# A depthwise convolution of 31 taps: half of it as streamed matrices on TensorE, half summed in PSUM, and a layer norm about a pivot

## What is computed

```
def conformer_conv_module(h, w_pw1, b_pw1, w_dw, b_dw, ln_g, ln_b, w_pw2, b_pw2):
    a, g = jnp.split(h @ w_pw1 + b_pw1, 2, axis=-1)
    u = a * jax.nn.sigmoid(g)
    u = causal_depthwise_conv(u, w_dw) + b_dw      # 31 taps per channel, over the tokens
    u = jax.nn.silu(layer_norm(u, ln_g, ln_b))     # mean and variance over the 1024 channels
    return u @ w_pw2 + b_pw2
```

## Time and profile before

| what | us |
|---|---|
| median of 3 runs | 2044.67 (2043.39 to 2046.08) |
| the profiled execution: time, span from first to last instruction | 2046.26, 2044.4 |
| busy in it: TensorE, VectorE, GpSimd, ScalarE | 1964.0, 905.4, 1159.7, 440.5 |
| chain that ended last: TensorE, VectorE, ScalarE | 81%, 10%, 2% |
| mean granted clock of TensorE | 0.98 of full speed |

### The profile page before, as it was taken

The page is one execution under the profiler, slowest core; times in us unless marked ns, Lnnn a source line. Parts: engine busy times, 40 slices in busy tenths (PEclk is TensorE's granted clock), DMA queues, the critical chain, the costliest instruction groups (busy, mean ns, idle before and its releaser), DMA issues.

```text
span 2044.4 us, 24823 instructions
## 1 busy us (share of the span) xinstructions
PE 1964.0 (96%) x8961; PEld 1542.2 (75%) x8961; DVE 905.4 (44%) x1383; ACT 440.5 (22%) x954; POOL 1159.7 (57%) x648
## 2 busy tenths in 40 slices
PE   8999899999999999999999999997879999999998
PEld 6876567888888877877788888876657678888886
DVE  6345863543430055343543332118999453333202
ACT  3334641211110020033211110003253431111000
POOL 6963536766675556621676666646610367666662
PEclk9999999999999999999999999999989999999999
DMA  5431002223233213210243233222210123333311
GB/s 193 133 115 32 1 1 83 82 92 94 93 121 99 76 46 100 93 42 13 71 115 101 93 104 110 85 73 63 72 31 0 35 69 113 92 92 108 109 61 41
DMA packets 42376, 160.85 MB, mean 79 GB/s; under 512 B 4928, under 2 KB 5184, under 8 KB 42304
## 3 DMA queue, kind: packets, MB, share of 16 engines
q1 hardware_dynamic: 41472, 157.74, 24.8%
q10 hardware_dynamic: 832, 2.11, 0.3%
HBM read 157.73 MB, written 2.10 MB: 78 GB/s over the span
## 4 chain that ended last, share of the span: by engine, by line
PE 81%; DVE 10%; ACT 2%; issue 1%; POOL 0%; POOLq 0%; DVEq 0%; ACTq 0%
PE psum L467 24%; PE psum L468 24%; PE psum L469 24%; DVE y_dw L1692 5%; PE psum L499 1%; PE psum L643 1%; PE psum L657 1%; PE psum L719 1%; PE psum L520 1%; PE psum L737 1%; DVE e_ring L1331 1%; PE psum L526 1%; PE psum L539 1%; DVE glu L1675 0%; PE psum L684 0%
## 5 line engine op out<-in xcount | busy, mean ns | idle before, releaser
L404 POOL TENSOR_TENSOR w_lo<-raw,w_hi 128x1024 fp32r<-128x1024 f32 (+1 forms) x277 | 732.6, 2645 | 23.1
L401 POOL TENSOR_SCALAR w_hi<-raw 128x1024 fp32r<-128x1024 f32 (+1 forms) x277 | 317.6, 1147 | 720.5 <-PE psum L469 686.7
L467 PE MATMUL psum<-h_hi,w_hi 128*128 128x512 f32 x1704 | 682.1, 400 | 35.4 <-DVE tmp L1671 20.0
L468 PE MATMUL psum<-h_lo,w_hi 128*128 128x512 f32 x1704 | 677.8, 398 | 0.0
L469 PE MATMUL psum<-h_hi,w_lo 128*128 128x512 f32 x1704 | 677.6, 398 | 0.0
L467 PEld LDWEIGHTS psum<-h_hi,w_hi 128*128 128x128 f32 x1704 | 323.3, 190 | 119.4 <-issue 31.6
L469 PEld LDWEIGHTS psum<-h_hi,w_lo 128*128 128x128 f32 x1704 | 322.8, 189 | 78.4
L468 PEld LDWEIGHTS psum<-h_lo,w_hi 128*128 128x128 f32 x1704 | 323.2, 190 | 76.8
L467 PE MATMUL psum<-g_hi,w_hi 128*128 128x512 f32 x528 | 208.8, 396 | 0.0
L468 PE MATMUL psum<-g_lo,w_hi 128*128 128x512 f32 x528 | 208.8, 396 | 0.0
L469 PE MATMUL psum<-g_hi,w_lo 128*128 128x512 f32 x528 | 208.8, 396 | 0.0
(11 more groups left out here) (242 smaller groups left out, 1810.4 us busy)
## 6 DMA issues: line engine op xcount, KB each, us to landing
raw<-in_wide SPq DMA_DIRECT2D x229, 512.0 KB, 3.5
raw<-in_down SPq DMA_DIRECT2D x48, 704.0 KB, 4.1
x<-in_xt ACTq DMA_DIRECT2D x4, 512.0 KB, 7.3
out<-x SPq DMA_DIRECT2D x8, 256.0 KB, 2.0
o_diff<-in_angles SPq DMA_DIRECT2D x1, 512.0 KB, 6.2
cols<-in_cols SPq DMA_DIRECT2D x1, 221.0 KB, 4.6
tabs<-in_tables SPq DMA_DIRECT2D x1, 208.0 KB, 5.4
k_fox<-forget ACTq DMA_DIRECT2D x8, 2.0 KB, 2.0
```

The lines of the kernel that those rows point to most:

```text
L401: nc.gpsimd.tensor_scalar(w_hi[:, slot, 0:w], raw[:, j % RAW, 0:w], 1.0, 1.0, ALU.mult, ALU.mult)\
L404: nc.gpsimd.tensor_tensor(w_lo[:, slot, 0:w], raw[:, j % RAW, 0:w], w_hi[:, slot, 0:w].bitcast(F32), ALU.subtract).then_inc(units_split, 1)
L467: pe.matmul(out_ap, lhs[0], rhs[0], start=first, stop=False)
L468: pe.matmul(out_ap, lhs[0], rhs[1], start=False, stop=False)
```

## The change

Chunks 0 to 3 stay on VectorE, chunks 4 to 7 are TensorE's. VectorE's taps keep their running sum in a PSUM bank (TAP_BANK); only the last tap of a chunk writes y_dw in SBUF. Chunks 2 and 3 begin their sum with the bias less the pivot, so they are centred when their last tap is in.

For TensorE the scaled identities go. The host lays out, for each half chunk of 64 channels, a weight unit of eight 128x128 tiles (`tap_tiles`): its 128 rows hold the 64 channels twice, the second time shifted by SHIFT = 8 tokens, and its 128 columns hold two sums of the same channels, of taps 0 to 14 and of taps 15 to 30. Eight such units are loaded, split and multiplied like any other, 24 matmuls each. ScalarE writes the operand in both shifts (`place`: a copy of the high part to PSUM, and eight copies of 64 partitions), and moves the half sum that must be shifted by REACH = 15 tokens into y_dw (`move`); VectorE adds the other half and the bias (`conv_out`, two operations of 64 partitions a chunk).

The layer norm takes the mean over the channels of chunk 0 as its pivot as soon as chunk 0 is convolved (`pivot`, one matmul), every chunk is centred by it when it is done, and squares are taken then. GpSimd adds up chunks and squares of the first six (`add_chunk`), between splits of weights; TensorE sums the columns of these two sums and of the last two chunks; the mean is taken off the squares' mean and, by `less_mean`, off each chunk. The sigmoid goes to PSUM. The core of the diff:

```diff
+CONV_DVE, CONV_PE = (0, 1, 2, 3), (4, 5, 6, 7)
+CONFORMER = ["g0", "v0", "g1", "v1", "g2", "v2", "g3", "v3", "g4", "v4", "g5", "v5", "c4a", "c4b",
+             "g6", "v6", "c5a", "c5b", "g7", "v7", "c6a", "c6b", "c7a", "c7b"]
+LN_ORDER = (0, 4, 1, 5, 2, 6, 3, 7)
+SUM_AFTER = {1: 19, 2: 20, 3: 23, 4: 24, 5: 28}
-CONV_PE = (5, 6, 7)
-DIAGONALS = 40
...
+            def add_chunk(k):
+                c = LN_ORDER[k]
+                pool.wait_ge(centred, k + 1)
+                nc.gpsimd.tensor_tensor(total[:], (y_dw[:, LN_ORDER[0], :] if k == 1 else total[:]), y_dw[:, c, :], ALU.add)\
+                    .then_inc(sum_added, 1)
+                pool.wait_ge(ln_squared, k + 1)
+                nc.gpsimd.tensor_tensor(square_sum[:], square_sum[:], squares[:, k % 2, :], ALU.add).then_inc(squares_added, 1)
...
-            with n.loop(pe, 3, units_split=4, group=4):
-                for u in range(4):
-                    feature_unit(h_of, bank=next_bank())
-            conv(0)
-            add_means(0, 3)
...
+            for name in CONFORMER[OPEN:]:
+                if name[0] == "c":
+                    conv_unit(int(name[1]), "ab".index(name[2]))
+                else:
+                    feature_unit(h_of, bank=next_bank())
+                if name == "v5":
+                    pivot()
+            pe.wait_ge(sum_added, LN_BY_POOL - 1)
+            ln_add(total, 0, first=True)
+            pe.wait_ge(squares_added, LN_BY_POOL - 1)
+            ln_add(square_sum, 1)
+            for k in range(LN_BY_POOL, KC):
+                pe.wait_ge(centred, k + 1)
+                ln_add(y_dw[:, LN_ORDER[k], :], 0)
+                pe.wait_ge(ln_squared, k + 1)
+                ln_add(squares[:, k % 2, :], 1, last=k == KC - 1)
...
+            gate(6)
+            place(6)
+            ln_square(1)
+            ln_square(2)
+            move(5)
+            gate(7)
+            place(7)
             load_sqrt()
+            ln_square(3)
+            move(6)
+            ln_square(4)
+            ln_square(5)
+            move(7)
...
-                        v.scalar_tensor_tensor(y_dw[:, c, :], glu[:, c, k:k + S], col("w_dw", c * TAPS + k), y_dw[:, c, :],
-                                               ALU.mult, ALU.add).then_inc(conv_chunk if k == TAPS - 1 else tapped, 1)
+                        v.scalar_tensor_tensor(y_dw[:, c, :] if last else acc, glu[:, c, k:k + S], col("w_dw", c * TAPS + k), acc,
+                                               ALU.mult, ALU.add).then_inc(done, 1)
...
+            glu_chunk(6, 1)
+            conv_taps(10)
+            conv_out(5)
+            conv_taps(3 * TAPS - n.base["taps"])
+            conv_taps(6)
+            glu_chunk(7, 1)
+            conv_taps(11)
+            conv_out(6)
+            conv_taps(4 * TAPS - n.base["taps"])
+            conv_out(7)
```

More of the change, by code:

```diff
@@ L900, in _ @@
             swiglu()
[L902 to L916, removed]
@@ new lines, in pivot, with ln_add @@
+            def pivot():
+                pe.wait_ge(conv_chunk, 1)
+                pe.matmul(psum[:, PIVOT_BANK, :], ones[:], y_dw[:, LN_ORDER[0], :], start=True, stop=True).then_inc(pivot_added, 1)
+            def ln_add(source, place, first=False, last=False):
+                for b in range(NB):
+                    mm = pe.matmul(psum[:, STAT_COL, 4 * place + b:4 * place + b + 1], source[:, b * P:(b + 1) * P], ones[:, 0:1],
+                                   start=first and b == 0, stop=last and b == NB - 1, skip_group_check=True)
+                mm.then_inc(ln_columns, 1)
@@ new lines, in _ @@
+            for c in range(5):
+                gate(c)
+            place(4)
+            gate(5)
+            place(5)
+            move(4)
+            ln_square(0)
+            gate(6)
[5 more added lines that the diff above has]
+            place(7)
+            load_sqrt()
+            ln_square(3)
[3 more added lines that the diff above has]
+            move(7)
+            ln_square(6)
+            ln_square(7)
@@ L1708, in _ @@
-            conv_taps(142, CONV_PE[0] * TAPS)
-            conv_out(2)
-            dve.wait_ge(row_added, n.take("row_added", KC))
-            for c in range(KC):
-                v.scalar_tensor_tensor(y_dw[:, c, :], psum[:, STAT_COL, :], -1.0 / D, y_dw[:, c, :], ALU.mult, ALU.add)\
-                    .then_inc(centred, 1)
-            row_stat(EPS_LN, STAT_ROW)
+                        if c - 1 in CENTRED_WHOLE:
+                            dve.wait_ge(centred, LN_ORDER.index(c - 1) + 1)
+                        elif c:
+                            dve.wait_ge(conv_chunk, c)
@@ new lines, in conv_out @@
+            def conv_out(c):
+                j = c - CONV_PE[0]
+                for g in range(2):
+                    rows = slice(g * HD, (g + 1) * HD)
+                    bank = group()
+                    dve.wait_ge(conv_moved, 2 * j + g + 1)
+                    v.scalar_tensor_tensor(y_dw[rows, c, :], bank[rows, :], cols[rows, COL["b_dw"] + c:COL["b_dw"] + c + 1], y_dw[rows, c, :],
+                                           ALU.add, ALU.add).then_inc(evacuated, 1)
+                dve.wait_ge(evacuated, n.now("evacuated"))
+                centre(c)
@@ new lines, in _, with less_mean @@
+            dve.wait_ge(mean_ready, 1)
+            v.scalar_tensor_tensor(ln_less[:], ln_mean[:], -1.0, ln_mean[:], ALU.mult, ALU.mult).then_inc(ln_step, 1)
+            dve.wait_ge(ln_step, 2)
+            v.tensor_tensor(variance[:], variance[:], ln_less[:], ALU.add).then_inc(ln_step, 1)
+            dve.wait_ge(rooted, n.take("rooted"))
+            v.reciprocal(scale_col[:], root[:]).then_inc(col_ready, 1)
+            def less_mean(c):
+                v.tensor_tensor(y_dw[:, c, :], y_dw[:, c, :], psum[:, HIGH_BANK, :], ALU.subtract).then_inc(mean_taken, 1)
```

255 lines of the change are left out of this document (154 added, 101 removed).

## The result

| | us |
|---|---|
| before, four runs beside the changed kernel | 2045.27 (2043.39 to 2046.08) |
| changed, four runs | 1996.49 (1991.58 to 1999.52) |
| ratio of the two | 0.976, 95% interval 0.9738 to 0.9783 |
| the profiled execution of the changed kernel: time, span | 1999.52, 1997.7 |

The change makes the kernel 2.4% faster, 49 us. The forecast was 1997.0 with a range of 1986 to 2013. On another chip the pair stood at 1997.24 to 2043.74 us, a ratio of 0.9772 (0.9759 to 0.9786).

A forecast was written before the change was run, and what follows sets the result against it. VectorE's taps were taken to bound the convolution stage. VectorE to 1532, GpSimd to 1539.5, column sums to 1545.5 and the norm put w_out at 1551.5, 47.9 us earlier: 1997 us, range 1986 to 2013.

The forecast's parts named there:

- The size of the whole: Whole kernel: time moves as w_out's first matmul does, from 1599.35 to 1551.5, 47.9 us earlier, giving 1997 us.
- The tap: VectorE's convolution taps with the sum in PSUM: 0.786 us each start to start, 99.0 us for 126.
- Rival B: VectorE's taps: the running sum in PSUM costs more, 0.88 to 0.99 us a tap, time 2006 to 2017; chance 0.17.
- VectorE's row: VectorE's work in the convolution stage, summed as one chain from 1401.0: 131.0 us, last chunk centred at 1532.
- GpSimd last: End of the stage: GpSimd's additions and splits end at 1539.5, 7 us later than VectorE's last centring.
- The tail: TensorE's column sums after GpSimd's end: five groups at 0.84, 4.2 us, plus 1.8 for the clock, ending 1545.5.
- From mean to the first normed chunk: Layer norm after the column sums: mean, variance, root, reciprocal, spreading and handovers, from 1545.5 to 1548.4.
- Rival D: VectorE's taps still stall beside GpSimd, 32 to 40 us of delay, time 2029 to 2037; chance 0.06.
- Rival C: End of the stage: GpSimd is not late, w_out starts behind the last square at 1540, time 1985; chance 0.11.
- Rival E: TensorE's clock stays low in the stage, w_out starts at 1628, time 2073, slower than before; chance 0.04.
- A to D: The four faster cases: the forecast itself (0.62), Rival B (0.17), Rival C (0.11), Rival D (0.06); total stated as 0.95.
- The opening argument: Stage from 1400 to 1600 us: VectorE's taps hold 46.8% of the chain of waits, so VectorE bounds the stage.

The follow-up runs named there:

- e0: The changed kernel run again without edits, on the chip of the first lot of follow-up runs: 1997.24 us.
- e1: The changed kernel with GpSimd's additions of chunk 5 placed four splits earlier in its list: 1986.30 us.
- e6: The changed kernel leaving out 8 of the 31 taps of one VectorE chunk, so part of the sum is missing: 1997.35 us.
- e4: The changed kernel with one part undone, VectorE's taps keeping their running sum in SBUF as before: 2044.45 us.
- e5: The kernel before with one part of the change alone, all chunks' taps on VectorE with their running sum in PSUM: 2015.96 us.
- e7: e1 leaving out 8 of the 31 taps of one VectorE chunk, so part of the sum is missing: 1986.12 us.
- e3: e1 with three filler matmuls, whose results nobody reads, before the column sums of each of the last two chunks: 1986.79 us.
- e2: The changed kernel with 26 filler matmuls, whose results nobody reads, in TensorE's wait before the column sums: 2001.73 us.

## Why the prediction was right, step by step

- **The size of the whole.** 1997.0 forecast, 1996.49 and 1997.24 measured. w_out's first matmul was forecast at 1551.5 and stands at 1553.90 and 1551.65 in two profiles (47.9 forecast; 45.5 and 47.7). That w_out's start carries the whole difference holds to 1.2 us.
- **The tap.** Taken at 0.786 start to start from L1257 and L1692; twelve in a row take 9.46, 0.79 each. Rival B (0.88 to 0.99) is excluded on the reading and on the writing side: 756 ns with the sum read from PSUM and written there, 748 where it is only read there. Right. The up to 130 ns more that were estimated from the Trainium skill, Perfetto Trace Analysis, "Optimizing Scalar/DVE Operations", don't show for this form; the measurement decides.
- **VectorE's row.** Forecast 1532, measured 1529.1 (1526.8 in e0). The chunk that starts at 1401.54 was forecast at 1401.7, and the waits are 2.4 us (0.17 at the first sigmoid, 2.21 for TensorE at the third chunk) against 2.0. The table load that I saw in the 1.6 us of before doesn't delay the first GLU. A GLU operation is followed after 0.66 us (1406.61 to 1407.27), not 0.79, since the next one doesn't need its output: eight times, 1.0 us. The rest of the 3 us I did not take apart.
- **GpSimd last.** Forecast: it ends 1539.5, 7 us behind VectorE. Measured: 1536.94, 7.8 behind. Two stalls were named, ahead of v7 and of c7b; both are there (15.45 and 7.33 us, for squares), and the second ends at 1513.45 where I had 1515 for the square. TensorE waits 3.0 us at v7, with 4 forecast, and 2.1 more at c7b, which I had not counted. e1 (-10.9 us) and e6 (0) show it as the cause; it had been argued only. How much of it is the place of the additions and how much ScalarE's late squares is not separated: e1 moves the additions and leaves both waits for squares as they were.
- **The tail.** This is the term that was mis-sized: five groups at 0.84 and 1.8 for the clock, 6.0 in all, from 1539.5 to 1545.5. There were six groups at 1.71, 10.3 us from 1535.78 to 1546.1. I had taken the low clock as a passing surcharge; it holds through all six groups (granted 0.50). The group that I left out is that of `total`, which starts 0.1 us behind the start of GpSimd's last addition and runs beside it, so it only counted once the groups were slower than the additions. Past GpSimd's end the sums took 9.2 us and not 6.0.
- **From mean to the first normed chunk.** 2.9 forecast; 1546.21 to 1550.67 is 4.5, again at the low level: the two spreadings of eight matmuls take 2.07 and 1.91. By terms, -2.6 (GpSimd), +3.2 (sums), +1.6 (this one) and +0.2 behind it make the 2.4 us between 1551.5 and 1553.90; the total is better than its parts, and that is luck.
- **Rival D** was priced wrongly. Were the delay still there, the time would be 2044.45 (e4) and not 2029 to 2037, and no gain at all would be left: a split costs the taps 2.7 us and not the 1.6 of its sum. Its chance of 0.06 was argued from maxima that e4 and e5 bear out.
- **Rival C** (GpSimd not late, 1985) is about what e1 makes of the kernel, 1986.3, though by another way: C wanted earlier squares, and e1 has earlier additions. **Rival E** didn't come: until 1489 the granted clock is 1.00 and TensorE without a gap. The chances of A to D add up to 0.96, where the prediction's last sum has 0.95; nothing hangs on it.

The opening argument said that VectorE is what the stage waits for. This was right and hid the reason: by e5, its row shrinks by 29.6 us with not one instruction less, and by e4 the moved work would only have brought more stalls, since every matrix of taps is one more split: 58 us of them, where there were 25.5 before.

## What to carry to other kernels

Read a line's maximum beside its median before moving work off an engine: if the maximum is several times the median while another engine is busy, the stall is the cost, and work that adds instructions to that other engine can eat the whole gain (2044.45 against 1997.24 here). An accumulator of VectorE that is kept in PSUM cures it for operations with one other input in SBUF, at no cost in the operation itself. And when the engine that set the end gives way, lay the next engine's list against it in order: two additions that stood four splits too late were worth 11 us. The length of a wait on such an engine is no measure of what it is worth: with the additions early, 22.8 us of GpSimd's waits for squares turned into 16.4 for VectorE, and no gain showed.

## What the runs showed of the hardware

- GpSimd and VectorE take turns when a tap reads two tensors from SBUF: two taps and one split in 4.26 us, where they take 1.57 and 3.49 alone.
- A small operation of VectorE can wait as long as a large one. ln_less, 128x4 with both inputs in SBUF, lasts 0.16 us in the changed kernel, where GpSimd is idle, and 1.91 (e7) and 2.21 us (e3) beside the second instruction of a split, with which it ends to within 0.02 us.
- A group of four one-column matmuls starts 0.81 to 0.90 us after the one before at 2.4 GHz and 1.71 at 1.2. In e7, where TensorE had no wait, the level fell during the fourth such group in a row (0.95, 1.03, 1.03 us, then 1.42, then 1.85); in e2 during the sixth, behind 22.48 us of fillers; in the changed kernel it was low from the first, behind a wait of 11.65 us.
- An fp32 matmul of 512 columns stands in the trace as two records of 0.43 us at full clock. A filler of that kind costs 0.86 us.
